# A hybrid attention and MLP layer on eight cores: one exponential over two neighbouring score banks, in pairs of tiles

## The reference

```python
u = rms_norm(x, norm_mix)
# u @ w_in -> q_n, k/v of three branches, gates, q_f, k_f, v_f, f_l
o_n = gate0 * compressed_attention(...)  \
    + gate1 * selected_block_attention(...) \
    + gate2 * sliding_window_attention(...)        # 8 heads in 2 groups, WINDOW = 512
o_f = softmax(q_f @ k_f.T / 8 + csum_t - csum_s, causal) @ v_f     # 8 heads, forgetting gate
y = g_a * (o_n @ w_branch_nsa) + g_b * (o_f @ w_branch_fox)
h = x + y @ w_out
h = h + square(relu(rms_norm(h) @ w_up)) @ w_down
out = rms_norm(h)
```

## Time and profile before

| | us |
|---|---|
| median of 3 runs | 1206.81 |
| the three runs | 1202.40, 1206.81, 1234.30 |
| the profiled execution | 1204.45 |
| its span, from the first to the last instruction, slowest core | 1201.9 |
| spans of the eight cores | 1195.7 to 1201.9 |

### The profile page before, as it was taken

One profiled execution on the slowest core, in us unless ns is written; L12 is line 12 of the kernel. 1 busy time (PEld: TensorE's weight loads), 2 busy tenths in 40 slices (PEclk: granted clock), 3 DMA queues, 4 the chain that ended last, 5 costly groups with the idle time before them and its releaser, 6 DMA issues.

```text
span 1201.7 us, 25510 instructions; the slowest of 8 cores (1195.7 to 1201.9 us)
## 1 busy us (share of the span) xinstructions
PE 1148.5 (96%) x8991; PEld 629.0 (52%) x8991; DVE 619.9 (52%) x1306; ACT 631.7 (53%) x1264; POOL 67.6 (6%) x127
## 2 busy tenths in 40 slices
PE   3988988999999999999999999999999999999997
PEld 2555566676676666754444445444444444444443
DVE  2546667642434434333344366447565565747467
ACT  5655789999998999962222266430212112020354
POOL 0000223111110000000000000000000000000000
PEclk9989999999999999999999999999999999999999
DMA  9953040002020020442041040422211121111034
GB/s 217 235 102 61 7 70 19 3 2 40 3 39 5 4 37 20 107 140 79 11 71 36 1 89 1 88 40 49 53 36 35 35 36 36 36 35 36 1 117 164
DMA packets 18362, 65.91 MB, mean 55 GB/s; under 512 B 4320, under 2 KB 4704, under 8 KB 14016
## 3 DMA queue, kind: packets, MB, share of 16 engines
q0 software_dynamic: 4752, 34.61, 16.2%
q1 hardware_dynamic: 13488, 29.69, 8.0%
HBM read 90.30 MB, written 8.39 MB: 82 GB/s over the span
## 4 chain that ended last, share of the span: by engine, by line
PE 88%; DMA 4%; DVE 4%; issue 3%; ACT 1%; DVEq 0%; POOL 0%; ACTq 0%; SPq 0%
PE bank L327 88%; DMA RG<-x 4%; DVE RG L327 3%; ACT RG L327 1%; DVEq L167 0%; DVEq L160 0%; DVE uT L327 0%; POOL RG L327 0%; ACTq L167 0%; SPq L167 0%
## 5 line engine op out<-in xcount | busy, mean ns | idle before, releaser
L327 ACT ACTIVATE RG<-bank 128x512 bf16<-128x512 f32 (+3 forms) x888 | 460.6, 622 | 349.4 <-PE bank L327 344.8
L327 PE MATMUL bank<-uT,arena 128*128 128x512 bf16 x2048 | 491.0, 379 | 2.4 <-DMA arena<-wall 2.3
L327 PE MATMUL bank<-RG 128*128 128x65 bf16 (+8 forms) x3860 | 350.1, 228 | 16.7 <-DVE RG L327 13.5
L327 PEld LDWEIGHTS bank<-uT,arena 128*128 128x128 bf16 x2048 | 199.6, 98 | 215.5 <-issue 3.1
L327 DVE TENSOR_TENSOR RG<-RG,bank 128x512 f32<-128x512 f32 x320 | 218.8, 686 | 144.3 <-PE bank L327 140.9
L327 PE MATMUL bank<-arena,RG 128*128 128x512 bf16 x1280 | 279.5, 379 | 0.0
L327 PEld LDWEIGHTS bank<-RG 128*128 128x128 bf16 (+3 forms) x3860 | 205.1, 98 | 105.8 <-issue 23.9
L327 PEld LDWEIGHTS bank<-arena,RG 128*128 128x128 bf16 x1280 | 124.6, 98 | 148.3
L327 DVE TENSOR_TENSOR RG<-RG 128x512 bf16<-128x512 f32 (+3 forms) x203 | 120.4, 593 | 155.4 <-ACT RG L327 150.8
L327 ACT ACTIVATE RG<-RG 128x512 f32<-128x512 f32 (+3 forms) x149 | 86.5, 585 | 73.4 <-DVE RG L327 46.7
L327 DVE CAST RG<-bank 128x128 bf16<-128x128 f32 (+3 forms) x132 | 60.0, 457 | 89.3 <-PE bank L327 88.0
(11 more groups left out here) (34 smaller groups left out, 235.2 us busy)
## 6 DMA issues: line engine op xcount, KB each, us to landing
arena<-wall POOLq DMA_DIRECT2D x32, 1024.0 KB, 10.0
RG<-x SPq DMA_DIRECT2D x32, 512.0 KB, 13.6
out<-RG SPq DMA_DIRECT2D x32, 256.0 KB, 2.1
RG<-c_qx SPq DMA_DIRECT2D x8, 144.0 KB
RG<-wall POOLq DMA_DIRECT2D x1, 1024.0 KB, 13.5
RG<-RG SPq DMA_DIRECT2D x48, 4.0 KB, 1.8
RG<-c_kx SPq DMA_DIRECT2D x4, 144.0 KB
RG<-c_kx SPq DMA_DIRECT2D x8, 64.0 KB, 1.8
```

Source lines behind the costliest of these rows:

```text
L327: return P.emit(eng, lambda e, method=method, kw=kw: getattr(e, method)(**kw), ins, outs, inc)
```

## The change

Score banks 0 to 3 become two tensors of two banks each, `wide0` and `wide1`. Tiles are taken in pairs: tile 2k goes to the first bank of its tensor and is shifted to the bank's right end if it is narrow, tile 2k+1 to the second bank from its left end. So the columns of a pair lie side by side, and one exponential covers both. `PT` becomes 5 buffers of 1024 columns (before: 8 of 512). The masks, the scores and the `PV` matmuls keep their shapes and number.

```diff
-        for i in range(8):
+        for i in range(2):
+            P.own('wide%d' % i, 4096, bank=True)
+        for i in range(4, 8):
             P.own('bank%d' % i, 2048, bank=True)
-        banks = [ctx.enter_context(nc.psum_tensor('bank%d' % i, [128, 512], F32)) for i in range(8)]
+        wide = [ctx.enter_context(nc.psum_tensor('wide%d' % i, [128, 1024], F32)) for i in range(2)]
+        banks = [wide[i // 2][:, i % 2 * 512:i % 2 * 512 + 512] for i in range(4)]
+        banks += [ctx.enter_context(nc.psum_tensor('bank%d' % i, [128, 512], F32)) for i in range(4, 8)]
...
-        NPT = 8
+        NPT = 5
-        PT = [cv.alloc([512], BF16) for _ in range(NPT)]
+        PT = [cv.alloc([1024], BF16) for _ in range(NPT)]
...
             if i0 == 0:
+                W.pump(n=1)
                 P.dma('sp', prm[:, :], prm_d)
...
-        W.pump(n=3, after=[x_tok[5]])
+        W.pump(n=3, after=[x_tok[4]])
...
-            for t in range(n):
-                now[0] = t
-                tiles[t]['EXP']()
-                if t + depth < n:
-                    tiles[t + depth]['S']()
...
+            scores(0)
+            scores(1)
+            for k in range((n + 1) // 2):
+                now[0] = 2 * k
+                a = place(2 * k)
+                b = 512 + (tiles[2 * k + 1]['cols'] if 2 * k + 1 < n else 0)
+                E('act', 'activation', out=PT[k % NPT][:, a:b], in_=wide[k % 2][:, a:b], func=AF.Exp)
+                scores(2 * k + 2)
+                scores(2 * k + 3)
+                for t in (2 * k, 2 * k + 1):
+                    if t < n:
+                        fill(t)
+                    finish(t - LAG)
```

More of the change, by code:

```diff
@@ L45, in own @@
     def own(self, name, nbytes, bank=False):
-        n = 1 if bank else (nbytes + CELL - 1) // CELL
+        n = nbytes // 2048 if bank else (nbytes + CELL - 1) // CELL
         q = 1 if bank else 4
@@ L55, in rects @@
         if m[0]:
-            return m, ((0, 1, 0, 1),)
+            es = 4 if ap.dtype == F32 else 2
+            width = m[1].shape[1] * 2048 // es
+            lo = ap.offset % width
+            hi = lo + sum(d[0] * (d[1] - 1) for d in [tuple(x) for x in ap.ap][1:])
+            return m, ((0, 1, lo * es // 2048, hi * es // 2048 + 1),)
         es = 4 if ap.dtype == F32 else 2
@@ L702, in unit_tiles, with S @@
                 d['pe'] = cols / 2400.0 + 0.003 * len(segs) + sum(m[2] for m in masks) / 2300.0 + cols / 128 * (0.0295 if nv == 65 else 0.043)
[L704 to L708, removed]
+                d['cols'] = cols
+                def S(sb_, o, segs=segs, masks=masks):
+                    base = o
                     for j, (i, q0, n) in enumerate(segs):
@@ L714, in S, with PV @@
                         end = j == len(masks) - 1
[L715 to L724, removed]
+                        E('pe', 'matmul', inc=end, out=banks[sb_][:, base + bo:base + bo + n], lhsT=identb[:, :], rhs=trib[:, mo:mo + n], start=False, stop=end, skip_group_check=True)
+                def PV(pt, o, segs=segs, idx=idx):
+                    lead = idx == 0
                     for j, (i, q0, n) in enumerate(segs):
                         for s in range(q0 // 128, (q0 + n) // 128):
-                            E('pe', 'matmul', inc=j == len(segs) - 1 and s == (q0 + n) // 128 - 1, out=Obv[ob][:, s, 0:nv], lhsT=PT[d['pt']][:, o:o + 128], rhs=v_fn(i),
-                              start=idx == 0 and o == 0, stop=last[s] == (idx, i), skip_group_check=True)
+                            E('pe', 'matmul', inc=j == len(segs) - 1 and s == (q0 + n) // 128 - 1, out=Obv[ob][:, s, 0:nv], lhsT=pt[:, o:o + 128], rhs=v_fn(i),
+                              start=lead, stop=last[s] == (idx, i), skip_group_check=True)
+                            lead = False
                             o += 128
-                d['S'], d['EXP'], d['PV'] = S, EXP, PV
+                d['S'], d['PV'] = S, PV
                 if idx == len(tl) - 1:
@@ L766, in run_pipeline, with place, scores, finish @@
                 room[t] = room[t + 1] + max(tiles[t]['act'] - tiles[t]['pe'], 0.0)
[L767 to L772, removed]
-            for t in range(n):
-                now[0] = t
-                tiles[t]['EXP']()
-                if t + depth < n:
-                    tiles[t + depth]['S']()
+            if n % 2:
+                tiles.append(None)
+            def place(t):
+                return 512 - tiles[t]['cols'] if t % 2 == 0 else 0
+            def scores(t):
+                if t < n:
+                    tiles[t]['S'](t % 4, place(t))
+            def finish(t):
+                if 0 <= t < n:
+                    d = tiles[t]
+                    d['PV'](PT[t // 2 % NPT], place(t) + t % 2 * 512)
+                    for f in d['post']:
+                        f()
+            def fill(t):
                 d = tiles[t]
@@ L797, in run_pipeline @@
                     late = [f for f in late if f.groups]
[L798 to L801, removed]
+            scores(0)
[8 more added lines that the diff above has]
+                for t in (2 * k, 2 * k + 1):
+                    if t < n:
+                        fill(t)
+                    finish(t - LAG)
+            for t in range(n - LAG - 1, n):
+                if t >= (n + 1) // 2 * 2 - LAG:
+                    finish(t)
             while emit_one(n) is not None:
```

## The result

The changed kernel takes 1210.03 us (median; 1208.71 to 1213.14) against 1205.06 for the kernel before, measured beside it. The ratio is 1.005 with a 95% interval of 1.0036 to 1.0064. Two of the seven executions of the kernel before (1234.30 and 1279.70 us) fell in a slower state that hits executions of any of these kernels, and the ratio leaves such executions out (the median of the other five is 1203.59 us). So the change is slower, by about 6 us and by more than the measurement's uncertainty, though inside the 2% that were called no change. The predicted 1206 us was no move at all; the range of 1196 to 1217 holds the time.

What follows compares the result with a forecast made beforehand. PE is busy 96%; ACT sets the pace only where fillers run out. Uncovered -2, window part +1.5 and +2.5, covered 0, start +0.3, front -0.3: +2.0 on the profiled 1204.45 us, said as 1206, range 1196 to 1217.

Steps and rivals of the forecast that it cites:

- The price of the exponential: On ACT, a 1024-column exponential takes 1.04 us alone and 0.93 in a row, saving 0.045 us per pair.
- Rival 3: An exponential across two banks costs more than 1.10 us in a row; at 1.2 us +38 us, 1242; chance 0.04.
- The filler blocks: Window part: behind each of eight filler blocks ACT idles 1.57 us, 0.3 more than before, +2.5 us in all.
- The window part: 109 to 214 us, 88 pairs of tiles: +1.5 us for PE-ACT hand-overs, +2.5 for filler blocks.
- the chain: Scores and exponentials waiting on each other: 0.92 us per plain pair, 0.99 in the window part, +1.5 us there.
- The DVE waits stay: PE's waits for DVE, 13.7 us from 109 to 526 us, stay, since DVE's own work is the same.
- The uncovered stretches: 276 to 290, 349 to 362, 491 to 526 us, fillers run out: 64 pairs save 2.9 us, taken as -2.
- The covered stretches: 214 to 276, 290 to 349, 364 to 490 us: fillers keep PE full and ACT waits; change 0.
- The hand-over: Between PE and ACT: 0.10 us from PE to ACT, and 0.10 taken as an estimate for the way back.
- Rival 2: Pair hands over too late: blocks 0.8 us each, 0.08 per window-part pair more; +13 us, 1218; chance 0.16.
- Rival 1: Saving comes through in full on 152 window and uncovered pairs, no loss at blocks: -7 us, 1197; chance 0.22.
- The front: Before the attention part: earlier `TM` delays x tiles by what it gains; -0.3 us for the DMA engines' idle start.

Runs made afterwards that it cites:

- a_waits: The change with PE's waits on DMA queues put ahead of its waits on other engines: 1205.69 us, ratio 1.0039 to the kernel before.
- a_two_exp: The change in pair order, each wide exponential split into two of one bank, each bank handed back by its own: 1201.41 us, ratio 0.9989.
- b_front: The kernel before with the change's two front edits alone (`TM` at once, `QN` after x tile 4): 1200.25 us, ratio 0.9988.

## Why the prediction was wrong

**The price of the exponential: right.** Alone the wide one takes 1.02 us (1.04 said). In the change single ones stand at this width:

```profile
110.54 1.02 ACT L331 ACTIVATE RG<-wide 128x1024 bf16<-128x1024 f32 x1 [0.69 <-PE wide L331]
```

In a row of plain pairs they start every 0.92 and 0.94 us in turn, 0.93 as said. Rival 3 (over 1.10 us) is out: reading two banks costs nothing extra that these rows show. The Trainium skill, "ScalarE: Activation LUTs", section "What ACT_TABLE_LOAD costs", gives 186 ns + 0.833 ns a column, from which I estimate 1.04 us alone; the trace has 1.02.

**The filler blocks: right in ACT's idle time, not in what it costs.** ACT's idle time behind the eight blocks of the window part is 1.79, 1.68, 1.54, 1.44, 1.27, 1.61, 1.33 and 1.54 us. The mean is 1.52 against 1.25 before, +0.27 each, 2.2 us in all; +0.3 and 2.5 were said, with 1.57 us of idle. Two of them:

```profile
125.91 1.94 ACT L331 ACTIVATE RG<-wide 128x1024 bf16<-128x1024 f32 x2 [1.68 <-PE wide L331]
...
162.35 4.03 ACT L331 ACTIVATE RG<-wide 128x1024 bf16<-128x1024 f32 x4 [1.54 <-PE wide L331]
```

**The window part: half.** +4.0 us were said (1.5 for the chain and 2.5 for the blocks), +2.0 measured. Nor did it grow where the sum had put it: behind all eight blocks the marks stand at +0.7 us (163 us) and at 206 us at +0.9, and the rest comes in one step between 206 and 211 us. "The DVE waits stay" failed here: from 109 to 214 us PE's waits for DVE fell from 10.7 to 4.7 us. I read this so: PE comes later to the output banks, and the delay of the blocks and the chain took the place of waits that PE had before.

**The uncovered stretches: the first failed step.** -2 us was said. Measured by marks near their ends: 273 to 296 us +1.0 (the marks there stand at 1.5 and 2.5; the covered stretch ahead of them had given back 0.5), 351 to 363 about +0.3, 493 to 525 +1.5. Of these 2.8 us, a_waits has 0.3 less in the first and 0.8 less in the last: those are the waits at first scores. The last head shows the rest best. The 34 tiles of the kernel before, the 17 pairs of the change (start, us, what, count):

```profile
507.75 16.12 ACT L327 ACTIVATE RG<-bank 128x512 bf16<-128x512 f32 x34 [0.27 <-PE bank L327]
```
```profile
514.62 16.15 ACT L331 ACTIVATE RG<-wide 128x1024 bf16<-128x1024 f32 x17 [1.21 <-PE wide L331]
```

Half as many instructions, and the same 16.1 us. Eleven plain pairs gain 0.05 each, as computed. But the three pairs with a 256-column tile keep the distance of the others (0.94, 0.90, 0.94 us), where before a narrow and a full tile took about 0.77. ACT could start the next one sooner, since it idles 0.09 to 0.13 us behind each of the three; the chain over PE doesn't let it. Two pairs behind masked tiles take 1.01 and 1.11. I had computed the chain (0.92 for a plain pair) and the gain of a plain pair, and then taken the gain for all 64 pairs with a small deduction. In this row the slow pairs eat up the whole gain of the plain ones, so the deduction for unit ends, 0.9 us, should have been the whole 2.9.

**The covered stretches: the second and larger failed step.** "0; two pairs take PE ... 2.2 us, above the chain's 1.84 to 2.05." Measured +0.5 from 296 to 351 and +4.4 from 363 to 493 us. The sum left out the eight places at which PE's own hand-over is not 0.1 but 0.4 to 1.2 us, the first scores of the heads: the edit of a_waits takes away 2.3 of these 4.4 us, and 4.2 of the 9.2 in all. For the other 2.1 us the reading is this, and no experiment separates it: that sum was an average, and the fillers are not laid evenly; where a slot has few or none, the pair is as bare as in an uncovered stretch. PE's waits for ACT in 34 places fit that. That both banks come back late and the start waits for both scores is what costs here too: a_two_exp, which has neither, loses 1.0 us in this stretch. The kernel before had the stalls at first scores in plain sight: its two waits of PE for ACT, 1.8 us together, stand in the earlier trace rows. I used that row only as a bound on what a faster ACT might gain, and never asked what the same stall costs with one pair ahead.

**The hand-over: slightly low.** 0.10 us each way were taken. By the semaphore events of the change, PE's next score most often starts 0.135 us after ACT's semaphore has its value. With it and the measured 1.02 us, the chain of a plain pair is 0.10 + 0.22 + 0.38 + 0.135 + 1.02 = 1.855 us for two, 0.93 each. That is as long as ACT's pace, so nothing is left to take up any delay.

**Rival 2** (the pair hands over too late, +13 us, chance 0.16) is what happened, at 9.2 us in the attention part, but by other terms: it put the price in the window part, and most of it fell behind 363 us. **Rival 1** had the chain against it, as the prediction said. **The front:** -0.3 was said, -1.4 measured in b_front. That the range of 1196 to 1217 held the time is luck in part: behind 212 us the attention part cost 7.2 us where a gain of 2 was said, and what kept the sum inside is that the window part came out 2.0 us cheaper than said and the front about 1.

## What to carry to other kernels

Merging two instructions saves the fixed part of one, but its input must be complete before it starts and its buffers come back only when it ends; price both delays on the chain, for the shortest pair as well as for the plain one, and only then the saving. Here, at 507 us, they cost 11.7 us and the saving gave back 4.1. A short stall of the feeding engine that now costs nothing is to be looked up and priced again when a change takes away the lead that hides it; and waits that are long satisfied belong ahead of the one that comes last.

## What the runs showed of the hardware

- A wait on a semaphore that already has its value still takes PE time: 0.11 to 0.12 us each. One wait for ACT and eight such waits ahead of one matmul took 1.07 us (change, 512.68 to 513.75 us), where a wait for ACT alone most often takes 0.135.
- One ACT instruction reads 1024 fp32 columns across two PSUM banks at the rate of one bank: 1.02 us alone against 0.60 for 512 columns, and 0.93 in a row against 0.98 for two of 512.
- In a row, the recorded duration of a 512-column exponential grows from one to the next while starts are 0.4775 us apart (0.634 us at 278.0 us, 0.884 at 287.4). The ends are 0.490 apart in the same row, and I take that for ACT's pace.
